# A transformer on one core: the last three down quarters by tile and column half, one weight split and the column sums moved behind the norm

## The reference

```python
def rms_norm(x, g):
    y = xf * lax.rsqrt(jnp.mean(xf * xf, axis=-1, keepdims=True) + EPS)
    return (y * g).astype(x.dtype)
def modulate(h, shift, scale):
    return h * (1.0 + scale[:, None, :]) + shift[:, None, :]
def swiglu(h, w_gate, w_up, w_down):
    return (jax.nn.silu(h @ w_gate) * (h @ w_up)) @ w_down
...
        y = jnp.concatenate([y_conv, y_nsa, y_sgu, y_pool], axis=-1) @ w_out[l]
        x = x + rms_norm_2(y, norm_mix_post[l])
        h = rms_norm_2(x, norm_ffn_pre[l])
        y = conv_ffn(h, ffn_up[l], ffn_conv_w[l], ffn_conv_b[l], ffn_down[l])
        x = x + rms_norm_2(y, norm_ffn_post[l])
```

## Time and profile before

| | us |
|---|---|
| median of 3 runs | 2026.15 (2019.21 to 2026.22) |
| profiled execution, own time | 2024.71 |
| its span | 2023.0 |
| PE busy | 1896.2 (94%) |
| DVE busy | 1425.4 (70%) |
| ACT busy | 938.0 (46%) |
| granted TensorE clock, mean | 0.957 |

### The profile page before, as it was taken

How to read it: one execution, slowest core, us unless ns; L and a number is a source line. 1 busy time by engine, 2 the same in 40 slices (tenths; PEclk the granted TensorE clock), 3 DMA queues, 4 the chain that set the end, 5 groups by cost and what they waited for, 6 DMA issues and landing times.

```text
span 2023.0 us, 32403 instructions
## 1 busy us (share of the span) xinstructions
PE 1896.2 (94%) x12022; PEld 1707.7 (84%) x12022; DVE 1425.4 (70%) x2139; ACT 938.0 (46%) x1341; POOL 302.2 (15%) x292
## 2 busy tenths in 40 slices
PE   2999999899999999999999899999889998979998
PEld 2998778799989998788889799877779986769996
DVE  6778788677877787667765655456669956657984
ACT  2444455444444444455454544444554345554443
POOL 1001010000110010000000000019612103931110
PEclk9999999899999999899999999988789999879999
DMA  9777765357787776344520554552155554124453
GB/s 364 255 274 275 264 230 206 119 195 277 272 306 249 272 284 236 119 185 182 180 95 1 185 187 177 194 180 84 64 171 184 187 188 145 63 83 139 176 187 122
DMA packets 61413, 382.13 MB, mean 189 GB/s; under 512 B 6896, under 2 KB 6896, under 8 KB 24448
## 3 DMA queue, kind: packets, MB, share of 16 engines
q1 hardware_dynamic: 41040, 300.96, 41.2%
q0 software_dynamic: 19856, 77.93, 11.2%
q10 hardware_dynamic: 432, 2.08, 0.3%
HBM read 379.89 MB, written 1.05 MB: 188 GB/s over the span
## 4 chain that ended last, share of the span: by engine, by line
PE 87%; DVE 8%; ACT 2%; issue 2%; DMA 1%; SPq 0%; DVEq 0%; ACTq 0%
PE ps L490 13%; PE ps L491 13%; PE ps L492 13%; PE ps L456 12%; PE ps L458 11%; PE ps L457 11%; PE ps L530 1%; PE ps L555 1%; DMA arena<-in_mod 1%; PE ps L768 1%; PE ps L882 1%; DVE ring_lo L1463 1%; PE ps L790 1%; PE ps L777 1%; PE ps L915 1%
## 5 line engine op out<-in xcount | busy, mean ns | idle before, releaser
L1463 DVE TENSOR_TENSOR ring_lo<-ring,w_hi 128x1024 fp32r<-128x1024 f32 x534 | 657.4, 1240 | 357.9 <-ACT w_hi L1064 354.2
L1064 ACT ACTIVATE w_hi<-ring 128x1024 fp32r<-128x1024 f32 x556 | 586.4, 1059 | 651.0 <-PE ps L492 329.2
L490 PE MATMUL ps<-h_lo,w_hi 128*128 128x256 f32 x2112 | 603.2, 286 | 9.6 <-issue 5.7
L491 PE MATMUL ps<-h_hi,w_hi 128*128 128x256 f32 x2112 | 602.1, 285 | 0.0
L492 PE MATMUL ps<-h_hi,ring_lo 128*128 128x256 f32 x2112 | 602.0, 285 | 0.0
L490 PEld LDWEIGHTS ps<-h_lo,w_hi 128*128 128x128 f32 x2112 | 410.3, 194 | 11.6 <-issue 7.2
L491 PEld LDWEIGHTS ps<-h_hi,w_hi 128*128 128x128 f32 x2112 | 410.4, 194 | 0.0
L492 PEld LDWEIGHTS ps<-h_hi,ring_lo 128*128 128x128 f32 x2112 | 410.1, 194 | 0.0
L456 PE MATMUL ps<-w_hi,h_lo 128*128 128x512 f32 x632 | 263.3, 417 | 24.4 <-DVE h_lo L1850 6.4
L458 PE MATMUL ps<-w_hi,h_hi 128*128 128x512 f32 x632 | 255.0, 404 | 0.0
L457 PE MATMUL ps<-ring_lo,h_hi 128*128 128x512 f32 x632 | 255.0, 404 | 0.0
(11 more groups left out here) (319 smaller groups left out, 2041.0 us busy)
## 6 DMA issues: line engine op xcount, KB each, us to landing
ring<-in_stream SPq DMA_DIRECT2D x278, 1024.0 KB, 4.8
arena<-in_mod POOLq DMA_DIRECT2D x128, 512.0 KB, 5.7
arena<-in_mod SPq DMA_DIRECT2D x3, 2048.0 KB, 17.4
gate<-in_wide POOLq DMA_DIRECT2D x3, 1536.0 KB, 7.2
arena<-in_nsaw POOLq DMA_DIRECT2D x2, 1072.0 KB, 10.4
arena<-in_mod SPq DMA_DIRECT2D x1, 1536.0 KB, 26.6
arena<-in_konst POOLq DMA_DIRECT2D x1, 1295.5 KB, 6.4
arena<-in_mixw POOLq DMA_DIRECT2D x2, 576.0 KB, 11.7
```

Of the source, the lines that this page charges most:

```text
L490: nc.tensor.matmul(dst, hi, x_lo, start=(r == 0 and i == 0 and b % 2 == 0), stop=False)
L491: nc.tensor.matmul(dst, hi, x_hi, start=False, stop=False)
L1064: nc.scalar.activation(w_hi[:, q % SPLITS, :], ring[:, half % SLOTS, (q % 2) * QUARTER:(q % 2 + 1) * QUARTER], ACT.Copy).then_inc(w_hi_rea ...
L1463: v.tensor_tensor(ring_lo[:, slot, cs], ring[:, slot, cs], w_hi[:, q % SPLITS, :], ALU.subtract).then_inc(w_lo_ready, 1)
```

## The change

- `down_last` takes the last three quarters (`TAIL` = 3), after the low parts of all three: 18 matmuls for tile 0, then 9 for the first column half of tile 1, then 9 for the second, which signals one `quarter_done` after each quarter.
- The mixer outputs' chunks 5, 6 and 7 go through `down_last` too; it waits for `conv_out` before it asks for chunk 6's low part, ahead of any of its matmuls.
- ACT and DVE split one quarter fewer during each down product (up to the next phase's first); the next phase's second quarter is split at the start of `norm_parts` (all norms but 0 and 2).
- DVE's part of `mod_cols` stands behind `norm` instead of ahead of it in norms 1, 3 and 4. On PE the sums stay ahead of the transposes.
- `post_norm` begins with the one-element root, ahead of its first wait.

```diff
+TAIL = 3
...
-            def down_last(q, count, parts, bank):
-
-                for kk in (count - 2, count - 1):
+            def down_last(q, count, parts, bank, late=None):
+
+                tail = range(count - TAIL, count)
+
+                def three(kk, tt, i):
+                    slot, half, buf = ((q + kk) // 2) % SLOTS, ((q + kk) % 2) * QUARTER, (q + kk) % SPLITS
+                    x_hi, x_lo = parts(kk, tt)
+                    hi = w_hi[:, buf, i * 512:(i + 1) * 512]
+                    lo = ring_lo[:, slot, half + i * 512:half + (i + 1) * 512]
+                    dst = ps[:, bank + 2 * tt + i, :]
+                    nc.tensor.matmul(dst, x_lo, hi, start=False, stop=False)
+                    nc.tensor.matmul(dst, x_hi, lo, start=False, stop=False)
+                    return nc.tensor.matmul(dst, x_hi, hi, start=False, stop=(kk == count - 1))
+
+                for kk in tail:
+                    if late is not None and kk == late[0]:
+                        pe.wait_ge(late[1], late[2])
                     low_part(q + kk, None, 0)
...
+                    for i in range(2):
+                        mm = three(kk, 0, i)
+                mm.then_inc(part_done, 1)
+                for kk in tail:
+                    mm = three(kk, 1, 0)
+                mm.then_inc(part_done, 1)
+                for kk in tail:
+                    three(kk, 1, 1).then_inc(quarter_done, 1)
...
                 pe.wait_ge(no_out, l + 1)
                 out_chunk(4)
-                out_chunk(5)
-                pe.wait_ge(conv_out, l + 1)
-                out_chunk(6)
-                out_chunk(7)
+                down_last(BASE[f"mix{l}_out"], KC, lambda k, tt: h_parts(MIX_CHUNKS[k], tt), DOWN_BANK, (6, conv_out, l + 1))
...
             def norm_parts(m):
 
+                if m > 0 and m != 2:
+                    split(NORM_AT[m] + LEAD - 2, NORM_AT[m] + LEAD - 1)
...
-                split(q0 + 23, q0 + 24 + LEAD - 1)
+                split(q0 + 23, q0 + 24 + LEAD - 2)
 
             def post_norm(end, k, bank):
 
                 o = bank * 512
+                nc.scalar.activation(warm[:, :], eps_col, ACT.Sqrt)
                 act.wait_ge(part_done, 2 * (6 + k) + 1)
...
             ffn(0)
+            norm(1)
             mod_cols(0, [1], 2)
-            norm(1)
             norm_parts(1)
...
```

More of the change, by code:

```diff
@@ L499, in down @@
                 quarter(q + kk, None, 0, lhs, lambda i, tt: ps[:, bank + 2 * tt + i, :], lambda i: kk == 0, lambda i: kk == count - 1, kk == count - 1)
-            def down_last(q, count, parts, bank):
-                for kk in (count - 2, count - 1):
-                    low_part(q + kk, None, 0)
[L505 to L519, removed]
@@ L590, in ffn @@
                         gates(*GATES[f][kk])
-                    if kk < DOWNQ - 2:
+                    if kk < DOWNQ - TAIL:
                         down(q0 + UPQ, kk, DOWNQ, hid_parts, DOWN_BANK)
@@ L815, in attention_out @@
                         pe.wait_ge(oT_lo, OT_FOX + kk // 2 + 1)
-                    if kk < KC - 2:
+                    if kk < KC - TAIL:
                         down(BASE[name], kk, KC, h_parts, 4)
@@ L1121, in down_split @@
                     turned += 6
-                split(turned, q0 + DOWNQ + LEAD - 1)
+                split(turned, q0 + DOWNQ + LEAD - 2)
             def keep_hi(f, j, it):
@@ L1168, in ffn_conv @@
                 gelu(UPS - 1, None)
-                split(q0 + UPQ + 4, q0 + UPQ + DOWNQ + LEAD - 1)
+                split(q0 + UPQ + 4, q0 + UPQ + DOWNQ + LEAD - 2)
             def qkv(q0, z0, w0, bufs, groups):
@@ L1295, in attention_out @@
                     nc.scalar.activation(h_hi[:, 2 * b:2 * b + 2, :].rearrange("p c t -> p (c t)"), ps[:, b, :], ACT.Copy).then_inc(oT_hi, 1)
-                split(BASE[name] + 4, BASE[name] + 8 + LEAD - 1)
+                split(BASE[name] + 4, BASE[name] + 8 + LEAD - 2)
             def mixer(l):
@@ L1627, in ffn @@
                 rest = list(range(t0 + MOD_UP * UPS, t1)) if mod else []
-                for q in range(d0 + LEAD, d0 + DOWNQ + LEAD - 1):
+                for q in range(d0 + LEAD, d0 + DOWNQ + LEAD - 2):
                     if q == turned:
@@ L1714, in ffn_conv @@
                 join(UPS - 1, None)
-                split(d0 + 5, d0 + DOWNQ + LEAD - 1)
+                split(d0 + 5, d0 + DOWNQ + LEAD - 2)
             def angles(w):
@@ L2104, in _ @@
             ffn(1)
+            norm(3)
             mod_cols(1, [0], 4)
-            norm(3)
             norm_parts(3)
             ffn(2)
+            norm(4)
             mod_cols(1, [1, 2], 5)
-            norm(4)
             norm_parts(4)
```

## The result

The changed kernel takes 2007.68 us (median of 6 runs, 2004.93 to 2012.89) against 2026.12 for the kernel before (6 runs, 2019.21 to 2027.91): a ratio of 0.9915, 95% interval 0.9897 to 0.9933, so 0.85% faster (the two medians alone give 0.9909). A second set gave 2005.88 against 2024.84 (0.9909, 0.9886 to 0.9931). The profiled execution took 2004.93 us, 19.8 less than that of before.

A forecast was written before the change was run, and what follows sets the result against it. PE, busy 94% of the span, was taken as the bound, so only its idle or slow time could be won. Terms -4.5 -2.0 -3.3 +2.1 +2.6 = -5.2 on 2024.7 gave 2019.5 us, range 2012 to 2027.5.

The forecast's parts named there:

- the mixer's tail: Mixer outputs before norms 7, 9: last matmul (E) 4.14 later, chain behind 3.10 shorter; net +1.04 us each, +2.1 both.
- the +2.6 for one fall: In the mixers' new 4.5 us PE wait: one clock fall from 2.4 to 1.2 GHz, +2.6 us; bounds 0 and 5.2.
- plain: Boundaries at norms 5 and 6: DVE starts the second column half 1.0 us sooner; gain 1.0 us, twice 2.0.
- post-normed boundaries: After an ffn (norm 8, end): transposes 5.04 us after last matmul, not 6.71; gain 1.67 us, twice 3.3.
- Norms 1, 3, 4: Column sums run on PE while DVE normalises: the transposes' waits of 1.45, 1.46 and 1.61 us go, gain 4.5 us.
- The moved split: In `norm_parts`: DVE's subtraction fits before `h_lo` with 0.8 us cover; taken 0, up to 9.8 us over eight boundaries.
- the ring loads: SP's queue: second last half released 1.36 us before the last matmul, not 5.44; expected cost nothing.
- rival A: Clock helps: no fall in mixers, nor in plain boundaries before the next phase; -13.0, 2011.7 us; chance 0.23.
- B: Boundaries give nothing: moved subtraction ahead of `h_lo` in eight boundaries, or tail late; +9.8, 2029.3 us; 0.15 with another rival.
- C: Mixer tail: clock falls in both 4.5 us waits, stays 1.2 GHz through 36 matmuls; +8.5, 2033.2 us; chance 0.07.

## Why the prediction was wrong

**Read wrongly, and shown: the mixer's tail.** The sentence "Now the tail asks for `conv_out` and then for the last quarter's low part before chunk 5 starts" is false, and so is the section on the change where it has the tail begin "after the low parts of all three" and the wait for `conv_out` "ahead of any of its matmuls". In the diff the loop over the halves stands inside the loop over kk: tile 0 of a quarter follows its own low part. So half of chunk 5 still covers the wait. E comes 1.5 us later, not 4.14; the chain shrinks by 3.07 (forecast 3.10); net -1.5 instead of +1.04 a mixer, and the wait of 1.7 us in place of 4.5 leaves the clock up, so the +2.6 for one fall is void too. These two terms make 7.8 us: the forecast's -5.2 becomes -13.0. The kernel that does what the forecast read takes 2019.12 us, and it has both the 4.65 us wait and the fall of the clock. The pricing was sound in the main; the object wasn't. That its time meets the forecast's 2019.5 so closely is partly luck. By its profile the forecast's terms come to -3.8 us (waits -14.3 and the end -1.6, together -15.9, forecast -16.0; `conv_out` to E +12.1, forecast +10.9 with one fall of the clock, where there were two shorter ones), and the other -2.2 us of its span lie in the transposes and phases that the forecast had no term for.

If only the misread tail is put right, the forecast is 2011.7 us. That is still 4 us above the measured time and just below the range's end, so a second term was missing (below).

**The terms of the plain and post-normed boundaries held.** Wait in norms 5 and 6: 2.37 (forecast 2.4); in 7 to 9: 5.07 (5.04); gain of norm 8 by its wait 1.63 (1.67). Norms 1, 3, 4: the waits of 1.45, 1.46 and 1.61 are gone, and the sums themselves took 0.1 to 0.8 us less. The moved split and the ring loads cost nothing that the list of PE's waits shows, as taken; the cover of the split was thinner (0.18 us) than the 0.8 that was worked out with slow transposes.

**Missing: the transposes' own length.** The forecast let the clock act on the matmuls behind a boundary only. But 16 transposes take 2.3 us at full clock and 3.7 at half, and with less idle before them they begin faster: 3.0 us less in norms 1, 3, 5 and 6 together, in the first profile. This and the phases behind make up the step from -13.0 to the -18.4 of the medians; rival A had the direction (given 0.23), and its 2011.7 is the nearest of the cases. It is the same number as the corrected forecast by chance: A kept the misread wait of 4.5 us and took 5.2 us off norms 5 and 6, where the first profile has 1.7 us of faster transposes. That the clock is the cause of such differences is shown by the fillers (11 us on the kernel before). How the last 5 us split between transposes, phases behind and scatter of medians isn't settled: single profiles differ by 1 us in one norm's transposes alone.

The parts by the medians: sums 5 to 10 us, tails 3.5, mixers' tail 3 to 5, early root 3 to 5; by the waits in the traces: sums 4.5, tails 3.4 (norms 5, 6 and 8), mixers' tail 0.6 given the root, root 1.2 given the tails. Only the intervals of the sums exclude that nothing was gained. Root and tails cover in part the same wait, so the parts don't add up to the whole.

**Rivals B and C**: the subtraction ran just in time, and no tail waited in the ffns, even with the low parts first, so B wasn't seen. C needed the 4.5 us wait. In the kernel that has it the clock did fall in both mixers, but it was back 4.2 and 3.8 us after the matmuls began, not after all 36.

## What to carry to other kernels

Before pricing a wait, write out the loop in the order in which the engine will issue it, indentation and all: what stands between the wait and the work it is said to block decides its price. Finish the output in the order in which the next chain needs it, and start the chain's first step before the last matmuls end. A wait on PE costs its length and can cost clock besides: a wait of 1.7 us cost none here, and one of 4.65 us about 2 us more in matmuls. Where PE must wait anyway, useless dense work in a free bank bought 7 to 11 us over five boundaries. And measure a part from a fixed event near it (here `conv_out`) to the next: that repeated to 0.06 us where whole phases and medians scattered by more than the effect.

## What the runs showed of the hardware

- Filling PE's waits of 2.4 to 8.1 us with 128x256 matmuls kept the granted clock at 1.0 through waits and transposes of all five boundaries; behind norm 5, where 2.3 us of idle were left, it fell. 16 fp32 transposes of 128x128 then take 2.30 us against 3.67 at 0.5.
- PE is fully busy by the profile in norm 4's 32 one-column fp32 sums (9 to 11 us), yet the clock fell 2.0 to 5.4 us after E in all 13 profiles without fillers there, and at 7.4 us with a 128x256 matmul after every fourth.
- The kernel before took 2014.7 to 2033.8 us in 51 executions, a scatter of 0.9%, while in the profiles of it and of its variants the waits before norms 5 to 9 repeat to 0.02 us where the code is the same. The time at 1.2 GHz moves with the device time: over the 51 executions the correlation is 0.77 (from each one's mean granted clock).
